# Second feed-forward up product by seven half-size block products in place of eight

## The reference

```python
h = _modulate(_rmsnorm(x, g_ffn[l]), sh2, sc2)                      # 512 x 1024
a = jnp.square(jax.nn.relu(jnp.einsum('bsd,df->bsf', h, w_ff1[l])))  # 1024 -> 4096
x = x + gt2[:, None, :] * jnp.einsum('bsf,fd->bsd', a, w_ff2[l])     # 4096 -> 1024
```

## Time and profile before

| | us |
|---|---|
| median of three runs | 1673.83 (1673.64 to 1673.90) |
| profiled execution | 1675.87 |
| its span, first to last instruction | 1673.1 |
| phase ff1b in it, first matmul to first matmul of ff2b | 431.69 to 518.73 |

### The profile page before, as it was taken

The page is one execution under the profiler, slowest core; times in us unless marked ns, Lnnn a source line. Parts: engine busy times, 40 slices in busy tenths (PEclk is TensorE's granted clock), DMA queues, the critical chain, the costliest instruction groups (busy, mean ns, idle before and its releaser), DMA issues.

```text
span 1673.1 us, 19977 instructions
## 1 busy us (share of the span) xinstructions
PE 1646.5 (98%) x7759; PEld 1314.4 (79%) x7759; DVE 1111.6 (66%) x1407; ACT 726.9 (43%) x1011; POOL 165.3 (10%) x158
## 2 busy tenths in 40 slices
PE   6999999999999999999999999999999999999999
PEld 3888778888888887887666788886678888888887
DVE  2888888532454577786999864548868886642364
ACT  2443334221222235646888523538832355431241
POOL 0005100000000000000455200004610000000000
PEclk9999999999999999999999999999999999999999
DMA  9544322222222242222111222221022222222222
GB/s 376 200 187 175 150 76 95 81 101 101 101 101 91 88 149 76 101 76 101 51 51 54 80 94 99 70 102 50 1 101 101 101 101 91 88 99 101 101 101 101
DMA packets 25422, 174.17 MB, mean 104 GB/s; under 512 B 2800, under 2 KB 3184, under 8 KB 5104
## 3 DMA queue, kind: packets, MB, share of 16 engines
q1 hardware_dynamic: 21440, 146.52, 24.4%
q10 hardware_dynamic: 3888, 26.38, 4.0%
HBM read 168.69 MB, written 4.19 MB: 103 GB/s over the span
## 4 chain that ended last, share of the span: by engine, by line
PE 83%; DVE 10%; ACT 5%; issue 1%; DMA 1%; ACTq 0%; POOL 0%; SPq 0%; DVEq 0%; POOLq 0%
PE bank L1608 25%; PE bank L1610 25%; PE bank L1609 25%; ACT p L381 3%; DVE p L1285 2%; DVE w_lo L863 2%; PE bank L2137 1%; PE bank L2163 1%; PE bank L2149 1%; DMA x<-x_in 1%; PE bank L1839 1%; DVE clipped L1259 1%; PE bank L1821 1%; PE bank L1657 1%; DVE t L962 1%
## 5 line engine op out<-in xcount | busy, mean ns | idle before, releaser
L1608 PE MATMUL bank<-h,w_hi 128*128 128x512 f32 x1184 | 465.5, 393 | 1.6 <-DVE w_lo L863 0.9
L1610 PE MATMUL bank<-h,w_lo 128*128 128x512 f32 x1184 | 460.9, 389 | 0.0
L1609 PE MATMUL bank<-h,w_hi 128*128 128x512 f32 x1184 | 460.8, 389 | 0.0
L381 ACT ACTIVATE w_hi<-raw 128x2048 fp32r<-128x2048 f32 (+1 forms) x129 | 246.6, 1912 | 312.4 <-DMA raw<-slabs 308.5
L863 DVE TENSOR_TENSOR w_lo<-raw,w_hi 128x2048 fp32r<-128x2048 f32 (+1 forms) x129 | 298.4, 2313 | 88.6 <-ACT w_hi L381 84.8
L1608 PEld LDWEIGHTS bank<-h,w_hi 128*128 128x128 f32 x1184 | 222.3, 188 | 49.2 <-issue 2.9
L1609 PEld LDWEIGHTS bank<-h,w_hi 128*128 128x128 f32 x1184 | 222.4, 188 | 47.1 <-issue 1.4
L1610 PEld LDWEIGHTS bank<-h,w_lo 128*128 128x128 f32 x1184 | 222.2, 188 | 46.4
L1608 PE MATMUL bank<-a_hi,w_hi 128*128 128x512 f32 x432 | 168.1, 389 | 0.3 <-DVE x L1537 0.3
L1610 PE MATMUL bank<-a_hi,w_lo 128*128 128x512 f32 x432 | 168.1, 389 | 0.0
L1609 PE MATMUL bank<-a_lo,w_hi 128*128 128x512 f32 x432 | 168.0, 389 | 0.0
(11 more groups left out here) (355 smaller groups left out, 2408.3 us busy)
## 6 DMA issues: line engine op xcount, KB each, us to landing
raw<-slabs SPq DMA_DIRECT2D x127, 1024.0 KB, 4.8
ada_chunk<-ada ACTq DMA_DIRECT2D x24, 1024.0 KB, 6.9
x<-x_in SPq DMA_DIRECT2D x4, 1024.0 KB, 9.1
spill_x<-x SPq DMA_DIRECT2D x1, 2048.0 KB, 10.5
x<-spill_x SPq DMA_DIRECT2D x2, 1024.0 KB, 6.0
out<-x SPq DMA_DIRECT2D x8, 256.0 KB, 2.0
raw<-slabs SPq DMA_DIRECT2D x2, 768.0 KB, 4.2
inv<-inv ACTq DMA_DIRECT2D x1, 1024.0 KB, 7.1
```

The costliest lines, as they stand in the source:

```text
L381: return act.activation(out, in_, f, **kw)
L1608: pe.matmul(out, w[0], a[0], start=start, stop=False)
L1609: pe.matmul(out, w[0], a[1], start=False, stop=False)
L1610: return pe.matmul(out, w[1], a[0], start=False, stop=stop)
```

## The change

Only `ff1b` changes its arithmetic. A slab is a 2 x 2 matrix of quarters: two halves of the output features by two halves of the inputs (4 tiles of 128 each); the activations are a 2 x 2 matrix of input halves by token halves (256 tokens). Seven products of such blocks give the four result blocks, in place of eight, with sums of blocks as operands:

- GpSimd makes the activation sums once, while `ff2a` runs, after it has added the high and low parts back together (`whole`), and makes three weight sums and one changed quarter for every slab (`weight_sums`: four operations of 512 numbers in a row).
- ScalarE makes the high parts in pieces: two quarters together, two sums, two quarters, the last sum (`plain_head`, `sum_heads`). It copies the first product out of PSUM, and does relu, square and high part of the finished tiles itself, one slab later (`a_head`).
- VectorE makes the low parts of the same pieces (`sum_tails`), adds the products together as they come (seven additions of a half bank and an SBUF row per slab), and makes the low parts of the activations two slabs later (`a_low`).
- TensorE runs 7 x 4 x 3 = 84 matmuls of 256 columns in a slab, in place of 48 of 512. The eight PSUM banks serve the products in turn.
- `ff2b` takes its first tile's inputs in pairs; several semaphores are merged or renamed, among them `gate_w_in`, which becomes part of `consts_in`.

In the order `seven_out` (ScalarE), `sum_tails` and `seven_sums` (VectorE), `weight_sums` (GpSimd), `seven_products` (TensorE):

```diff
+            def seven_out(n):
+                if n + 1 < 8:
+                    plain_head(n + 1)
+                act.wait_ge(sem("seven_done"), 6 * n + 1)
+                do.tell(fn(a_raw[:, 2 * n, left], seven_bank(n, 0), ACT.Copy), "first_taken", n + 1)
+                if n + 1 < 8:
+                    sum_heads(n + 1)
+                else:
+                    weight_head(SLAB0["ff2b"])
+                if n:
+                    a_head(2 * n - 2)
+                    a_head(2 * n - 1)
...
+            def sum_tails(n, parts):
+                for part in parts:
+                    if part < 2:
+                        dve.wait_ge(sem("sums_made"), 4 * n + 4 + (3, 2)[part])
+                        dve.wait_ge(sem("seven_head"), 4 * n + 6 + part)
+                        f, lo, hi = sum_place(n, ("s2", "s1")[part])
+                        do.tell(lows(lo, f, hi), "seven_split", 4 * n + 5 + part)
+                    elif part < 4:
+                        first = 2 * (part - 2)
+                        dve.wait_ge(sem("sums_made"), 4 * n + 8)
+                        dve.wait_ge(sem("seven_head"), 4 * n + (5, 8)[part - 2])
+                        do.tell(lows(quarter(w_lo, n, first, 2), quarter(raw, n, first, 2), quarter(w_hi, n, first, 2)),
+                                "seven_split", 4 * n + 5 + part)
+                    else:
+                        dve.wait_ge(sem("w_head"), SLAB0["ff1b"] + n + 1)
+                        f, lo, hi = sum_place(n, "s4")
+                        do.tell(lows(lo, f, hi), "w_split", SLAB0["ff1b"] + n + 1)
...
+            def seven_sums(n):
+                c11, c12, c21, c22 = (a_raw[:, 2 * n + m, side] for m in range(2) for side in (left, right))
+                if n:
+                    last_sum(n - 1)
+                if n > 1:
+                    a_low(2 * n - 4)
+                    a_low(2 * n - 3)
+                dve.wait_ge(sem("first_taken"), n + 1)
+                dve.wait_ge(sem("seven_done"), 6 * n + 2)
+                do.tell(dve.tensor_tensor(c12, seven_bank(n, 1), c11, ALU.add), "seven_read", 6 * n + 1)
+                if n + 1 < 8:
+                    sum_tails(n + 1, range(3))
+                dve.wait_ge(sem("seven_done"), 6 * n + 4)
+                do.tell(dve.tensor_tensor(c21, seven_bank(n, 3), c12, ALU.add), "seven_read", 6 * n + 2)
+                do(dve.tensor_tensor(c22, seven_bank(n, 2), c21, ALU.add))
+                do.tell(dve.tensor_tensor(c12, seven_bank(n, 2), c12, ALU.add), "seven_read", 6 * n + 3)
+                if n + 1 < 8:
+                    sum_tails(n + 1, range(3, 5))
+                else:
+                    weight_tail(SLAB0["ff2b"])
+                dve.wait_ge(sem("seven_done"), 6 * n + 5)
+                do.tell(dve.tensor_tensor(c11, seven_bank(n, 4), c11, ALU.add), "seven_read", 6 * n + 4)
+                dve.wait_ge(sem("seven_done"), 6 * n + 6)
+                do.tell(dve.tensor_tensor(c21, seven_bank(n, 5), c21, ALU.add), "seven_read", 6 * n + 5)
...
+            def weight_sums(n):
+                s = SLAB0["ff1b"] + n
+                pool.wait_ge(sem(f"raw_in{s % SLOTS}"), 16 * (s // SLOTS) + 16)
+                if n:
+                    pool.wait_ge(sem("tile_done"), 2 * (s - 2) + 2)
+                else:
+                    pool.wait_ge(sem("seven_split"), 4)
+                (s1, _, _), (s2, _, _), (s4, _, _) = (sum_place(n, which) for which in ("s1", "s2", "s4"))
+                q11, q12, q21, q22 = (quarter(raw, n, q) for q in range(4))
+                do.tell(pool.tensor_tensor(s1, q21, q22, ALU.add), "sums_made", 4 * n + 5)
+                if n == 7:
+                    pool.wait_ge(sem("seven_done"), 6 * 6 + 3)
+                do.tell(pool.tensor_tensor(s2, s1, q11, ALU.subtract), "sums_made", 4 * n + 6)
+                do.tell(pool.tensor_tensor(s4, q12, s2, ALU.subtract), "sums_made", 4 * n + 7)
+                do.tell(pool.tensor_tensor(q21, q11, q21, ALU.subtract), "sums_made", 4 * n + 8)
...
+            def seven_products(n):
...
+                pe.wait_ge(sem("seven_split"), 4 * n + 7)
...
+                one(0, of_quarter(0), tokens(low_k, left)).then_inc(sem("seven_done"), 1)
+                one(1, of_sum("s2"), mixed_tokens(1)).then_inc(sem("seven_done"), 1)
+                one(2, of_sum("s1"), mixed_tokens(0)).then_inc(sem("seven_done"), 1)
+                pe.wait_ge(sem("seven_split"), 4 * n + 8)
+                one(3, of_quarter(2), mixed_tokens(2)).then_inc(sem("seven_done"), 1)
+                one(4, of_quarter(1), tokens(high_k, left)).then_inc(sem("seven_done"), 1)
+                one(5, of_quarter(3), tokens(low_k, right)).then_inc(sem("seven_done"), 1)
+                pe.wait_ge(sem("w_split"), SLAB0["ff1b"] + n + 1)
+                one(6, of_sum("s4"), tokens(high_k, right)).then_inc(sem("tile_done"), 2)
```

More of the change, by code:

```diff
@@ L23 @@
 EPS = 1e-6
+HALF = S // 2
 H1, DH = 4, 128
@@ L303, in build, with seven_bank, seven_bank_free, sum_place @@
     first_banks, root_bank = [banks[n] for n in (4, 5)], banks[6]
+    def seven_bank(n, nth):
+        return banks[(7 * n + nth) % 8][:, 0:HALF]
+    def seven_bank_free(n, nth):
+        return ("first_taken", n + 1) if nth == 0 else ("seven_read", 6 * n + (1, 3, 2, 4, 5, 6)[nth - 1])
+    left, right = slice(0, HALF), slice(HALF, S)
+    low_k, high_k = slice(0, half_k), slice(half_k, KT)
+    def sum_place(n, which):
+        at_n = {"s1": (0, 3, 3), "s2": (1, None, 1), "s4": (2, None, 0)}[which][2 if n == 7 else n % 2]
+        if at_n is None:
+            tile = {"s2": 14, "s4": 15}[which]
+            return a_raw[:, tile, :], a_lo[:, tile, :], a_hi[:, tile, :]
+        return sum_raw[:, at_n, :], sum_lo[:, at_n, :], sum_hi[:, at_n, :]
+    def quarter(tensor, n, first, count=1):
+        return tensor[:, (SLAB0["ff1b"] + n) % SLOTS, S * first:S * (first + count)]
     up_banks = [(first_banks, banks[0:2], banks[6:8])[n % 3] for n in range(SLABS["upa"])] + [banks[0:2]] * SLABS["upb"]
@@ L581, in _ @@
             for half, name in enumerate(("ff1a", "ff1b")):
-                for t in range(16):
+                if half:
+                    for n in range(8):
+                        seven_out(n)
+                    a_head(14)
+                    a_head(15)
+                    weight_head(SLAB0["ff2b"] + 1)
+                for t in range(0 if half else 16):
                     tile_ready(name, t)
@@ L596, in _ @@
                 for n in range(8):
-                    weight_head(SLAB0[name.replace("1", "2")] + n + 2)
+                    if half == 0 and n == 5:
+                        mixed_heads()
+                    if half or n < 6:
+                        weight_head(SLAB0[name.replace("1", "2")] + n + 2)
+                    elif n == 6:
+                        plain_head(0)
+                        sum_heads(0)
                     if name == "ff1b":
@@ L918, in add_to_x @@
                                                          ALU.mult, ALU.subtract), "u_ready", first + m + 1)
-                    if (wide or m % 2) and not (total and m == KT - 1):
+                    if name == "ff2a" and m >= 6:
+                        if m == 6:
+                            sum_tails(0, range(5))
+                    elif (wide or m % 2) and not (total and m == KT - 1):
                         weight_tail(s + 2)
+                    if name == "ff2a" and m == 4:
+                        mixed_tails()
             def add_chunk(n):
@@ L1171, in _ @@
             for half, (up, down) in enumerate((("ff1a", "ff2a"), ("ff1b", "ff2b"))):
-                for t in range(16):
+                if half:
+                    for n in range(8):
+                        seven_sums(n)
+                    last_sum(7)
+                    for nth in (12, 13):
+                        a_low(nth)
+                    weight_tail(SLAB0["ff2b"] + 1)
+                    for nth in (14, 15):
+                        a_low(nth)
+                for t in range(0 if half else 16):
                     if 16 * half + t < 2:
@@ L1915, in _ @@
             for half in "ab":
-                product("ff1" + half, h_hi, h_lo, slabs=range(2 if half == "a" else 0, 8))
+                if half == "a":
+                    product("ff1a", h_hi, h_lo, slabs=range(2, 8))
+                else:
+                    for n in range(8):
+                        seven_products(n)
                 product("ff2" + half, a_hi, a_lo, 16, made=("a_ready", 0 if half == "a" else 16))
```

162 lines of the change are left out of this document (123 added, 39 removed).

## The result

The changed kernel takes 1676.88 us against 1674.03 for the kernel before (medians of 20 executions of each). Without three executions of the changed kernel that ran at a mean granted clock of 0.755, 0.58 and 0.755 and took 2057 to 2668 us, its median is 1676.74, 2.71 us longer than before, a ratio of 1.0016 [1.0008, 1.0023]. That is slower by a little under 0.2%. The forecast was 1.6 us longer.

A forecast was written before the change was run, and what follows sets the result against it. The prediction took ff1b to be bound by TensorE. Walking the engines' lists gave +0.50 us there, plus ff2b's stall of 1.1, so +1.6 on 1673.83: 1675.4 us, range 1669.0 to 1681.5.

The forecast's parts named there:

- TensorE's pace: In ff1b, 256-column matmuls start 0.120 us apart, so a slab of 84 takes 10.08 us in place of 10.88.
- The rival of slower matmuls: In ff1b, half-wide matmuls take 0.130 us in place of 0.120, giving +3.3 us, 1677.1; chance 0.06.
- The other engines' prices: Per ff1b slab: VectorE additions 0.424 us, low parts 0.692 and 1.226; GpSimd sums 1.28 each.
- The two engines hold each other up: In ff1b, VectorE's two-SBUF-input operations and GpSimd's exclude each other; a waiting sum costs VectorE at most 1.14 us.
- The rival with no hold-up: In ff1b, GpSimd and VectorE do not block each other: -4.8 us, 1669.0; chance 0.12.
- The rival with lighter sums: In ff1b, GpSimd's weight sums cost 1.04 us in place of 1.28: -2.4 us, 1671.4; chance 0.16.
- Two blocked low parts a round: In ff1b's slabs 3 to 5, VectorE waits twice for 0.96 us, making a round of 11.27 us.
- The last slab's scratch row: Slab 6 of ff1b takes 12.19 us: the last slab's second sum waits for slab 6's third product.
- ff2b's stall: At ff2b's 15th input tile, TensorE stalls 1.1 us because VectorE makes its low part behind the next slab's weights.
- the walk's +1.6: Engine lists followed through ff1b's eight slabs give +0.50 us; with ff2b's stall of 1.1, the sum is +1.6.
- The rest: ff2a's cover hides the activation sums, about 20.6 us; merged constants wait costs nothing; ScalarE's 8.2 us and DMAs fit.
- A worse alignment: Three or four of GpSimd's sums block VectorE in each ff1b round; third block +6.4 us; chance 0.24.

The follow-up runs named there:

- experiment 1: Changed kernel with each of GpSimd's four weight sums replaced by three fills that read no SBUF: 1669.45 us, ratio 0.9972 to the kernel before.
- experiment 2: Changed kernel with each of GpSimd's weight sums made a scaling of one input, still reading SBUF: 1668.50 us, ratio 0.9964 to the kernel before.
- experiment 4: Changed kernel, last slab's second weight sum waiting for slab 6's second product, only the third sum for the third: 1674.65 us, ratio 1.0003 to the kernel before.
- experiment 3: Changed kernel with VectorE's activation low parts 14 and 15 before the low part of ff2b's second weight slab: 1675.41 us, ratio 1.0007 to the kernel before.
- 6: Changed kernel with 8 small constant matmuls put into TensorE's wait before slab 7: 1675.73 us, ratio 1.0010 to the kernel before.
- experiment 8: Changed kernel with the edits of experiment 3 and experiment 4, and VectorE's round reordered, additions between low parts: 1670.94 us, ratio 0.9982 to the kernel before.
- experiment 10: Changed kernel with the edits of experiment 3 and experiment 4 and a third order of VectorE's round: 1672.89 us, ratio 0.9992 to the kernel before.
- the order alone: Changed kernel with only experiment 8's new order of VectorE's round: 1673.12 us, ratio 0.9993 to the kernel before.
- 5: Changed kernel with 14 small constant matmuls put before slab 7's first product: 1676.60 us, ratio 1.0014 to the kernel before.
- 7: Changed kernel with the edits of experiment 3 and experiment 4 together: 1673.06 us, ratio 0.9996 to the kernel before.

## Why the prediction was right, and where it was off

- *TensorE's pace.* 0.120 us a matmul: right, slabs 0 and 1 take 10.07 and 10.08. The rival of slower matmuls falls.
- *The other engines' prices.* Right where undisturbed: 0.424, 0.692, 1.226 and 1.30.
- *The two engines hold each other up.* Right, and shown by experiments 1 and 2: take the reads away, or make them lighter, and the round fits under TensorE. The rival with no hold-up is experiment 1's kernel: it came out 4.6 us under the kernel before, for a forecast of 4.8. The rival with lighter sums was priced at 1.04 us a sum; no run has that price, and experiment 2's sums of 0.62, 5.5 us under, lie beyond it. The exclusive lock of the Trainium skill (SBUF — State Buffer, "SBUF: two separate sides") holds here but for the 0.14 us that whoever waited gets back: 1.15 for a waiting sum against 1.30.
- *Two blocked low parts a round.* 11.31 against 11.27. Slab 2 was 0.23 longer than walked: its two activation low parts took 3.38 in place of 1.42, held up twice, so VectorE was done 0.42 later, while the hand-over to TensorE, set at 0.25, measures 0.06 (471.38 + 1.23 to 472.67).
- *The last slab's scratch row.* 12.22 against 12.19; shown by experiment 4.
- *ff2b's stall.* 1.12 against 1.1; shown by experiment 3.
- *Missing from the sum: TensorE's clock.* The forecast idled TensorE for 2.1 us before slab 7 and had it go on at full pace. The clock fell to half for 3.4 us, 1.3 us by experiments 4 and 6. With it the walk's +1.6 becomes +2.9, against 2.7 in the medians and 3.3 in the traces.
- *The rest* (ff2a's cover, the merged wait, ScalarE's lists, the DMAs): TensorE waited for none of it, as said.

A worse alignment was a fair rival: slab 2's extra block, the 11.45 of experiment 8 and experiment 10 show that a blocked low part more or less in a round, about 1 us, is decided by 0.03 to 0.2 us of who comes first. Such distances are no larger than the errors of the walk's own hand-over terms (0.19 in one of them), so that it caught the right number for this kernel's order was partly luck.

The account, in the profiled executions: seven products bring 6.4 us. Over 10.08 each, slabs 2 to 5 give back 4.9 us, what slabs 6 and 7 still have over it in experiment 4 is 0.8 and 0.3, the scratch row's wait is 12.22 - 10.86 = 1.4, the clock 1.3 and ff2b's order 1.1. These are 9.7, and 9.7 - 6.4 = 3.3. Why the medians have 0.6 less than that is not shown.

## What to carry to other kernels

When a change moves work onto GpSimd beside a busy VectorE, write down for each pair of instructions whether they exclude each other, and walk the two lists against each other; busy times alone, without the hold-ups, would have given this change a gain of 5 us (the prediction's 4.8). Put VectorE's work out of PSUM where GpSimd reads, and expect an order's value to be uncertain by a block a round until it is run. Then look at the two ends of the phase, where a shared scratch row and a list's order cost nearly as much here as all of the middle (3.8 us with the clock, against 4.9); and when a forecast has TensorE idle for 2 us before dense matmuls, price its clock as well.

## What the runs showed of the hardware

- TensorE's granted clock fell from 2.4 to 1.2 GHz behind an idle stretch of 2.04 us (505.35 to 507.51 less one pace) for 3.4 us, and in experiment 3's kernel behind 2.06 us; behind 1.59 us by the same measure (the order alone, 503.08 to 504.79) it did not. Matmuls of 256 columns start 0.21 us apart at the lower level, 0.12 at the upper.
- The mean granted clock recorded with each execution says how regular that is. One stretch of 3.4 us at half clock makes it 0.999, which 16 of the changed kernel's 17 compared executions show and 9 of 11 in experiment 3. With the idle stretch shortened or filled it is 1 of 11 (experiment 4), none of 11 (5 and 7) and 2 of 11 (6); with the order alone none of 11. The mean does not say where in the execution the clock fell.
- A long idle stretch is not the only occasion. In experiment 1's profile the clock fell for 3.4 us at 1145.8 us, behind idle stretches of 0.76 and 0.58 us; in the changed kernel's, the same two (0.76 and 0.59, before 1146.52 and 1151.87 us) left it at 1.00. Why it fell there is not shown. Of that experiment's seven executions the three with a mean of 0.999 took 1670.4 to 1670.5 us, the four with 1.000 took 1668.8 to 1669.5.
- A 128x128 float32 matmul that is not in three parts stands in the trace as two records of 0.109 us each.
- A GpSimd fill (0.527 us for 512 numbers) does not hold up VectorE's two-input operations; an operation of GpSimd with one input does (841 ns in place of 692 on average in experiment 2).
